# A limit on the bytes of transfers in flight, plain fp32 loads of the first inputs, and mixer weights cast straight into tiles

## The chip, the cores and the metric

The program runs on all 8 cores of one Trainium2 chip. Each core works on its own 2 of the 16 sequences and reads its own copy of the weights; nothing passes between cores. A time is the device time of one execution in microseconds (us), taken at the slowest core. The number to forecast is the median of such times.

## The reference

The reference is a trunk of two layers on x of shape 16 x 2048 x 1024, in fp32. Each layer adds half of a SwiGLU block, a token mixer, and half of a second SwiGLU block:

```python
for l in range(DEPTH):                                   # DEPTH = 2
    x = x + 0.5 * swiglu(rms_norm(x, ffn1_norm[l]), ffn1_w1[l], ffn1_w3[l], ffn1_w2[l])
    x = x + token_mixing(rms_norm(x, mix_norm[l]), w_in[l], ..., group_norm[l], w_out[l])
    x = x + 0.5 * swiglu(rms_norm(x, ffn2_norm[l]), ffn2_w1[l], ffn2_w3[l], ffn2_w2[l])
# swiglu(h, w1, w3, w2) = (silu(h @ w1) * (h @ w3)) @ w2, inner width 2816
```

`token_mixing` projects with `w_in`, splits the columns into four groups of heads (native sparse attention with a compressed, a selected and a windowed branch; a gated short convolution; sliding-window attention with sinks; a multi-scale pooling), normalises each group and projects with `w_out`.

## The kernel before

**Work and its units.** Activations lie with features on partitions and tokens on the free axis. A feed-forward (FFN) unit is one SwiGLU block on 1024 tokens of one sequence; there are 16 units, listed in `FL` (four of the first block of layer 0, then for each sequence two of its second block and two of the next layer's first, and so on). A mixer chunk is the token mixer on 512 tokens; there are 16, listed in `ML`. A unit's products are done in blocks of 512 columns with a scheme of seven products for each 2x2 block product (`PROD`, `prod`, L703): 11 "pairs" (columns of w1 and w3) and, per group of the inner width, four blocks of w2 (`dcq`). The sums of weight blocks that the scheme needs are formed on VectorE (DVE) by `wsum` (L659), those of activations by `tops` (L695).

**Weights.** They come as fp32 in DRAM (`w13r`, `w2r`, `winr`, `cw1r`, `wtokr`, `woutr`). An FFN tile of 128 x 2048 is cast to fp16 at first use by a DMA of GpSimd's queue (`prep`, L635), one sum is put in, and it is stored to a DRAM scratch (`s13`, `s2`) by SyncE's queue (L644); later units load it from there (`wload`, L670). The mixer's weights of a layer are cast from DRAM to a DRAM scratch (`hin`, `hcw`, `htok`, `hout`) by 32 DMAs on GpSimd's queue in `mix_scratch`, 6 of them spread over FFN unit 1 and the others over unit 2 of layer 0; what is not yet issued when the layer's first chunk begins is issued there in one go (`SCR.pop` in `mstream`). Every chunk then loads its tiles from that scratch (`proj` L860, `compress` L893, `chunk` L994, L995 and L1133).

**Inputs.** `norm` loads eight tiles of 128 x 512 tokens through GpSimd's queue, which casts them to fp16 (L605), squares them on ScalarE (L608), sums them by matmuls with ones (L610), and scales the tiles in place on DVE (L617). The first block of layer 0 reads `xT`; the result accumulates in `yT`, to which `ycopy` (L1358) copies `xT` by 32 DMAs from DRAM to DRAM on SyncE's queue.

**What sets the order.** The code first writes down all operations in program order, the FFN stream and the mixer stream interleaved by the table `MIX` (pairs of FFN units done and chunks done) and the work totals `tot`. `Graph.schedule` then runs a list scheduler over them with estimated durations: each engine takes the ready operation with the smallest key, within a look-ahead (`ahead`, `ahead_dma`, or an operation's own `look`) and within pools of tile slots. Operations that read PSUM get a smaller key by `bonus` or `bonusx`. DMAs are modelled as one pipe of `bw` bytes per us with a latency `hlat` (SyncE) or `slat` (GpSimd). The resulting order is fixed in the program; at run time only semaphores hold it back, and each queue issues strictly in its order. The pools matter below: 130 tiles "1" (128 x 520 fp16), 20 tiles "2" (128 x 1024 fp16 or 128 x 512 fp32), 7 tiles "4" (128 x 2048 fp16, a weight tile each).

## Time and profile before

| | |
|---|---|
| median of three runs, us | 4719.72 (lowest 4717.16) |
| profiled execution | 4709.09 us; its slowest core (core 3) spans 4708.1 us |
| other cores | 4670.8 to 4697.4 us |
| TensorE (PE) busy, core 3 | 4552.1 us, 97% of the span |
| DVE, ScalarE (ACT), GpSimd (POOL) busy | 3098.3, 3088.8, 897.1 us |
| HBM read and written | 630.62 and 256.43 MB |

How to read it: the profiled execution is 10.6 us, or 0.2%, faster than the median shown, so a saving read from it is taken off the median as it stands. PE's idle time in the profile is what a change of order can win or lose; the granted clock tells where PE ran below full speed.

### The profile page before, as it was taken

Reading aid. Unit: us, or ns where it says so; the run is one execution under the profiler, and the core shown is the slowest. Engines: PE = TensorE matmul, PEld = TensorE weight load, DVE = VectorE, ACT = ScalarE, POOL = GpSimd, SP = SyncE. Lnnn points to the kernel's source line nnn. Section 1 sums busy time; section 2 is a strip of 40 time slices with the busy share of each in tenths; the row PEclk is TensorE's granted clock in tenths of the full one; section 3 lists DMA queues with packets and bytes.
Section 4 is the critical chain, followed back from the end, with each engine's and each line's share of the span. In section 5 each row is a group of like instructions: output and inputs, shape, how many; then the busy total and the mean of one; then the engine's idle time right before and its main releaser. Section 6 shows DMA issues by size and latency. Waiting matters only on the chain.

```text
span 4708.1 us, 86069 instructions; the slowest of 8 cores (4670.8 to 4708.1 us)
## 1 busy us (share of the span) xinstructions
PE 4552.1 (97%) x25524; PEld 2109.0 (45%) x25524; DVE 3098.3 (66%) x7506; ACT 3088.8 (66%) x5770; POOL 897.1 (19%) x1328
## 2 busy tenths in 40 slices
PE   6999799999999999999999999999999999999989
PEld 2444344444444444444444444444444444444434
DVE  4747377657667667676667666766667776766553
ACT  3434277678686686786957586858685867767342
POOL 2021212021213112222112111121212221111101
PEclk8899899999999999999999999999999999999999
DMA  9898965766899649997567665674659996655634
GB/s 164 168 181 198 155 167 116 174 131 132 170 213 184 160 104 205 187 209 155 145 142 174 118 155 112 146 166 79 166 124 187 182 192 144 156 111 123 136 81 94
DMA packets 357974, 718.87 MB, mean 153 GB/s; under 512 B 37744, under 2 KB 149232, under 8 KB 356464
## 3 DMA queue, kind: packets, MB, share of 16 engines
q0 software_dynamic: 173392, 297.07, 44.0%
q1 hardware_dynamic: 184128, 416.29, 27.5%
q8 instruction: 219, 3.59, 0.3%
q14 instruction: 235, 1.93, 0.1%
HBM read 630.62 MB, written 256.43 MB: 188 GB/s over the span
## 4 chain that ended last, share of the span: by engine, by line
PE 87%; DMA 4%; DVE 3%; issue 2%; ACT 2%; another core or an unknown queue 1%; POOL 0%; SPq 0%; DVEq 0%; ACTq 0%; POOLq 0%
PE ps L703 62%; PE ps L864 8%; PE ps L1137 5%; PE ps L1152 4%; PE ps L1165 2%; DMA M<-s 2%; PE ps L610 1%; PE ps L1001 1%; DMA M<-w13r 1%; PE ps L1246 1%; PE ps L928 1%; DMA M<-yT 1%; DMA M<-w2r 0%; PE ps L968 0%
## 5 line engine op out<-in xcount | busy, mean ns | idle before, releaser
L703 PE MATMUL ps<-M 128*128 128x512 f16 x14784 | 3457.7, 383 | 84.0 <-DVE M L750 19.8
L703 PEld LDWEIGHTS ps<-M 128*128 128x128 f16 x14784 | 1414.4, 98 | 1782.9 <-issue 296.5
L659 DVE TENSOR_TENSOR M<-M 128x512 f16<-128x512 f16 (+1 forms) x1780 | 689.2, 411 | 181.7 <-DMA M<-s 83.4
L750 DVE TENSOR_TENSOR M<-M,ps 128x512 f16<-128x512 f32 x704 | 481.9, 685 | 458.8 <-PE ps L703 322.2
L802 POOL DMA_DIRECT2D yT<-M x464 | 400.7, 874 | 1685.3 <-ACT M L790 751.9
L754 ACT COPY M<-ps 128x512 f32<-128x512 f32 x704 | 411.2, 585 | 265.6 <-PE ps L703 259.9
L1155 ACT ACTIVATE M<-ps 128x512 bf16<-128x512 f32 x824 | 456.3, 604 | 38.6 <-PE ps L1152 34.6
L864 PE MATMUL ps<-M 128*128 128x512 f16 x1920 | 445.6, 379 | 0.4 <-DVE MS L1173 0.4
L710 ACT COPY ps<-ps 128x512 f32<-128x512 f32 x468 | 273.0, 583 | 249.5 <-PE ps L703 197.4
L695 DVE TENSOR_TENSOR M<-M 128x512 f16<-128x512 f16 x960 | 386.4, 421 | 35.3 <-DVE M L695 1.0
L742 DVE TENSOR_TENSOR M<-M,ps 128x512 f16<-128x512 f16 x352 | 240.8, 684 | 206.6 <-PE ps L703 203.0
L796 DVE SCALAR_TENSOR_TENSOR M<-ps,M 128x512 f32<-128x512 f32 x232 | 159.7, 689 | 232.6 <-PE ps L703 196.0
L864 PEld LDWEIGHTS ps<-M 128*128 128x128 f16 x1920 | 185.7, 98 | 217.4 <-issue 2.6
L617 DVE SCALAR_TENSOR_TENSOR M<-M,GN 128x512 f16<-128x512 f16 x384 | 263.8, 744 | 28.4 <-ACT M L624 27.8
L790 ACT ACTIVATE M<-ps 128x512 f32<-128x512 f32 x232 | 138.7, 599 | 217.8 <-PE ps L703 205.5
L1152 PE MATMUL ps<-M 96*128 96x512 f16 x824 | 273.6, 380 | 2.3 <-DVE M L1185 2.2
L738 ACT ACTIVATE M<-M 128x512 f16<-128x512 f16 x352 | 219.0, 631 | 82.4 <-DVE M L750 81.6
L734 ACT ACTIVATE M<-ps 128x512 f16<-128x512 f32 x352 | 209.5, 596 | 77.9 <-PE ps L703 74.6
L605 POOL DMA_DIRECT2D M<-yT x320 | 188.3, 667 | 343.5 <-PE ps L703 112.6
L608 ACT ACTIVATE M<-M 128x512 bf16<-128x512 f16 x384 | 228.6, 630 | 25.2 <-DMA M<-xT 11.7
L1165 PEld LDWEIGHTS ps<-M 128*128 128x128 bf16 x3296 | 176.4, 97 | 144.5 <-issue 28.3
L1137 PE MATMUL ps<-M 128*128 128x512 f16 x1024 | 235.7, 382 | 1.9 <-DVE M L1353 1.8
(152 smaller groups left out, 3983.7 us busy)
## 6 DMA issues: line engine op xcount, KB each, us to landing
M<-s SPq DMA_DIRECT2D x360, 512.0 KB, 4.9
yT<-M POOLq DMA_DIRECT2D x592, 256.0 KB, 7.8
s<-M SPq DMA_DIRECT2D x120, 512.0 KB, 8.0
M<-hin SPq DMA_DIRECT2D x240, 256.0 KB, 6.7
M<-w13r POOLq DMA_DIRECT2D x88, 512.0 KB, 13.0
M<-yT POOLq DMA_DIRECT2D x320, 128.0 KB, 7.5
M<-hout SPq DMA_DIRECT2D x128, 256.0 KB, 6.6
M<-w2r POOLq DMA_DIRECT2D x40, 512.0 KB, 9.9
```

What stands on the lines that cost most here:

```text
L659: op("dve", lambda e, o_=o_, a_=a_, b_=b_, al=al: e.tensor_tensor(out=wap(W, o_, w), in0=wap(W, a_, w), in1=wap(W, b_, w), op=al), reads=[ ...
L695: op("dve", lambda e, o_=o_, x_=x_, y_=y_: e.tensor_tensor(out=p1(o_)[:, 0:512], in0=p1(x_)[:, 0:512], in1=p1(y_)[:, 0:512], op=ALU.subtract),
L703: r = e.matmul(ps(bk)[:], lhsT=wap(w, pos, 128, j * 128), rhs=p1(B[n, k0 + j])[:, 0:512], start=start and j == 0, stop=stop and j == nk - ...
L710: op("act", lambda e: e.copy(out=ps(dst)[:], in_=ps(src)[:]), reads=[src], writes=[dst], dur=0.57)
L750: op("dve", lambda e: e.tensor_tensor(out=p1(dst)[:, 0:512], in0=p2f(t), in1=ps(bk)[:], op=ALU.add), reads=[t, bk], writes=[dst], dur=t_dv ...
L754: op("act", lambda e: e.copy(out=p2f(t), in_=ps(bk)[:]), reads=[bk], writes=[t], dur=0.6)
L802: op("pool", lambda e: e.dma_start(out=yT[s, :, dc, t0:t0 + 512], in_=p2f(o), accum_op=ALU.add), reads=[o], writes=[kY[s][dc][2 * u + hf]] ...
L864: r = e.matmul(ps(bk)[:], lhsT=p2(t)[:, kc * 128:(kc + 1) * 128], rhs=p1(xn[kc])[:, 0:512], start=kc == 0, stop=kc == 7, skip_group_check= ...
L1137: r = e.matmul(ps(bk)[:], lhsT=p2(wo)[:, kc * 128:(kc + 1) * 128], rhs=yap(kc), start=n == 0, stop=n == 7, skip_group_check=True)
L1152: op("pe", lambda e: e.matmul(ps(sbk)[:], lhsT=kap(), rhs=p4(Q)[0:kk, b * 512:(b + 1) * 512], start=True, stop=True, skip_group_check=True ...
L1155: op("act", lambda e: e.activation(out=p1b(et)[:, 0:512], in_=ps(sbk)[:], func=AF.Exp, scale=0.125), reads=[sbk], writes=[et], dur=0.65, t ...
L1165: r = e.matmul(ps(pb)[:, h * 65:(h + 1) * 65], lhsT=p1b(et)[:, h * 128:(h + 1) * 128], rhs=p1(V)[:, (kt % 4) * 130 + vi * 65:(kt % 4) * 13 ...
```

## The change

Five things change, and with them the order of the whole program.

1. The scheduler keeps a log of DMA bytes in the order of issue. A DMA is issued only when the bytes issued after some earlier DMA, its own included, would otherwise reach `win` = 5 MB: it then waits for that earlier DMA to land, in the model and by a semaphore on the chip. Bytes are those of the `dma` argument, which is the fp32 size for a cast.
2. For the units 0 to 2 (`XWIDE`: sequence 0, and the first 1024 tokens of sequence 1) `norm` loads `xT` as fp32 into tiles "2" by SyncE's queue, without a cast; squares and scaling read the fp32 tile and the scaled result goes to the fp16 tile. The loads of `norm` get a look-ahead of 400.
3. `mix_scratch` is gone. `mload` casts a mixer tile from the fp32 weights into the tile that the first chunk uses (GpSimd's queue) and stores it from there to the scratch (SyncE's queue); later chunks load it as before. `chunk` does the same with `wtokr`.
4. The scheduler's numbers: `ahead` 600 to 400, `hlat` 3 to 4, `slat` 6 to 4.5, `bonusx` 0 to 100, and shorter durations and larger byte counts for some DMAs.
5. The interleaving: the last point of `MIX` by which the mixer is done moves from 14.6 to 14.4 FFN units of 16, and the totals from 200 and 73 to 203 and 75.5.

```diff
-        self.ahead = 600
+        self.ahead = 400
-        self.hlat = 3.0
-        self.slat = 6.0
+        self.hlat = 4.0
+        self.slat = 4.5
+        self.win = 5000000.0
-        self.bonusx = 0
+        self.bonusx = 100
...
+                if c.dma:
+                    while dptr < len(dlog) and dcum + c.dma - dlog[dptr][0] >= self.win:
+                        dptr += 1
+                    q = dlog[dptr - 1][1] if dptr else None
+                    if q is not None and q.end > tnow + 1e-9:
+                        heapq.heappush(pe_, (q.end, c.i, c))
+                        continue
+                    throt[c.i] = q
...
+            if o.dma:
+                if throt.get(o.i) is not None:
+                    ex.add(throt[o.i])
+                dcum += o.dma
+                dlog.append((dcum, o))
...
-MIX, PREP, MS1 = ((2.0, 0.0), (5.0, 4.4), (14.6, 16.0)), (0, 1), 6
+LOOKX, XWIDE, XDMA = 400, (1, 2), 450e3
+MIX, PREP = ((2.0, 0.0), (5.0, 4.4), (14.4, 16.0)), (0, 1)
...
+            wide = src is xT and (s, c) < XWIDE
+            xf = [tile("2") for _ in range(8)] if wide else dst
+            xa = (lambda t: p2f(t)) if wide else (lambda t: p1(t)[:, 0:512])
             for kc in range(8):
-                op("pool", lambda e, kc=kc: e.dma_start(out=p1(dst[kc])[:, 0:512], in_=src[s, :, kc, c * 512:(c + 1) * 512]),
-                   reads=[kY[s][kc][c]], writes=[dst[kc]], dur=0.8, dma=262144)
+                op("sp" if wide else "pool", lambda e, kc=kc: e.dma_start(out=xa(xf[kc]), in_=src[s, :, kc, c * 512:(c + 1) * 512]),
+                   reads=[kY[s][kc][c]], writes=[xf[kc]], dur=0.45 if wide else 0.6, dma=262144 if wide else XDMA, look=LOOKX)
...
-        def mix_scratch(l):
...
+        def mload(l, kind, k, ap, wr, part=None):
+            src, dst, key = dict(hin=(winr, hin, kHIN), hout=(woutr, hout, kHOUT), hcw=(cw1r, hcw, kHCW))[kind]
+            nb = 128 * src.shape[-1] * 2
+            if (l, kind, k) in minscr:
+                op("sp", lambda e: e.dma_start(out=ap(), in_=dst[l, k]), reads=[key[l][k]], writes=[wr], dur=0.45, dma=nb, look=LOOKM)
+            else:
+                minscr.add((l, kind, k))
+                op("pool", lambda e: e.dma_start(out=ap(), in_=src[l, k]), writes=[wr], dur=0.6, dma=2 * nb, look=LOOKM)
+                op("sp", lambda e: e.dma_start(out=dst[l, k], in_=ap()), reads=[wr], writes=[key[l][k]], dur=0.45, dma=nb)
...
-                        spread(ms[:MS1], [1])
-                        spread(ms[MS1:], [2])
...
-                for f in SCR.pop(l, ()):
-                    f()
...
-        tot = [200.0 * max(1, len(FL)), 73.0 * max(1, len(ML))]
+        tot = [203.0 * max(1, len(FL)), 75.5 * max(1, len(ML))]
```

In the listings of the order below, lines of the changed kernel carry its own numbers: L627 is `norm`'s load (L605 before), L639 its scaling (L617), L657 and L659 the casts of FFN weights (L635, L637), L666 their stores (L644), L681 `wsum` (L659), L717 `tops` (L695), L725 `prod` (L703), L764 and L772 the readers of its PSUM banks (L742, L750), L824 the accumulation into `yT` (L802), L876 and L1022 the mixer casts, L1167 the projection with `w_out` (L1137), L1366 and L1378 the last steps of the pooling and of the group norm (L1336, L1348), L632 the sum of squares (L610).

**The program's start.** DVE's first instructions before, in which L659 are sums of weight tiles (four per tile) and L617 the scaling of the input tiles:

```order
L573 MEMSET EPSB 128x1
L576 MEMSET ONES 128x128
L659 TENSOR_TENSOR M<-M 128x512 x2
L617 SCALAR_TENSOR_TENSOR M<-M,GN 128x512 x8
L659 TENSOR_TENSOR M<-M 128x512 x2
L617 SCALAR_TENSOR_TENSOR M<-M,GN 128x512 x6
L742 TENSOR_TENSOR M<-M,ps 128x512
L617 SCALAR_TENSOR_TENSOR M<-M,GN 128x512 x2
L695 TENSOR_TENSOR M<-M 128x512 x16
L659 TENSOR_TENSOR M<-M 128x512 x5
```

DVE's first instructions now:

```order
L592 MEMSET EPSB 128x1
L595 MEMSET ONES 128x128
L681 TENSOR_TENSOR M<-M 128x512 x20
L639 SCALAR_TENSOR_TENSOR M<-M,GN 128x512 x8
L681 TENSOR_TENSOR M<-M 128x512 x8
L764 TENSOR_TENSOR M<-M,ps 128x512
L639 SCALAR_TENSOR_TENSOR M<-M,GN 128x512 x8
L717 TENSOR_TENSOR M<-M 128x512 x16
L772 TENSOR_TENSOR M<-M,ps 128x512 x3
```

The sums of five weight tiles stand ahead of the first eight scalings, and those of two more ahead of the second eight; before, it was half a tile and half a tile more.

SyncE's queue at the start before:

```order
L574 DMA GN<-fnorm 128x48
L1358 DMA yT<-xT 128x1024 x3
L644 DMA s<-M 128x2048
L1358 DMA yT<-xT 128x1024 x5
L644 DMA s<-M 128x2048 x19
L1358 DMA yT<-xT 128x1024 x2
L644 DMA s<-M 128x2048 x2
```

SyncE's queue now:

```order
L593 DMA GN<-fnorm 128x48
L627 DMA M<-xT 128x512 x9
L666 DMA s<-M 128x2048
L627 DMA M<-xT 128x512 x7
L666 DMA s<-M 128x2048
L1388 DMA yT<-xT 128x1024
L666 DMA s<-M 128x2048 x3
L1388 DMA yT<-xT 128x1024 x3
L666 DMA s<-M 128x2048
```

The sixteen input loads stand at the head of this queue, two stores among them, and the copies of `xT` to `yT` follow behind; GpSimd's queue now begins with 22 casts of weight tiles in a row.

**The start of the mixer.** GpSimd's queue where the first chunk of layer 0 begins, before (`hcw`, `htok`, `hin` and `hout` are the DRAM scratch, L802 the accumulation of FFN outputs):

```order
L851 DMA hcw<-cw1r 16x4096 x2
L802 DMA yT<-M 128x512
L851 DMA hcw<-cw1r 16x4096 x2
L852 DMA htok<-wtokr 32x8576
L848 DMA hin<-winr 16x8192 x3
L802 DMA yT<-M 128x512
L848 DMA hin<-winr 16x8192
L802 DMA yT<-M 128x512
L848 DMA hin<-winr 16x8192 x4
L802 DMA yT<-M 128x512
L848 DMA hin<-winr 16x8192 x6
L854 DMA hout<-woutr 16x8192 x8
```

The same place now:

```order
L876 DMA M<-cw1r 128x512 x5
L824 DMA yT<-M 128x512 x3
L659 DMA M<-w2r 128x4x384
L824 DMA yT<-M 128x512 x3
L876 DMA M<-winr 128x1024
L876 DMA M<-cw1r 128x512 x2
L824 DMA yT<-M 128x512
L876 DMA M<-cw1r 128x512
L1011 MEMSET M 128x8
L1022 DMA M<-wtokr 128x268
L1011 MEMSET M 128x8
L1048 MEMSET M 32x512
```

The 27 casts of the first listing, close behind each other, are replaced by those of the compression weights, of a projection tile and of the token projection; most projection tiles come later, and the eight of `w_out` come last.

**The end of the last mixer chunk.** PE's last instructions before:

```order
L864 MATMUL ps<-M 128x512 x16
L703 MATMUL ps<-M 128x512 x7
L864 MATMUL ps<-M 128x512 x16
L1348 MATMUL ps<-M,ONES 128x512 x2
L610 MATMUL ps<-M,ONES 128x512 x8
L1336 MATMUL ps<-M,PRB 128x512 x2
L1348 MATMUL ps<-M,ONES 128x512 x2
L703 MATMUL ps<-M 128x512 x8
L1137 MATMUL ps<-M 128x512 x64
L703 MATMUL ps<-M 128x512 x12
L610 MATMUL ps<-M,ONES 128x512 x8
L703 MATMUL ps<-M 128x512 x904
```

PE's last instructions now:

```order
L1167 MATMUL ps<-M 128x512 x16
L725 MATMUL ps<-M 128x512 x52
L1167 MATMUL ps<-M 128x512 x8
L725 MATMUL ps<-M 128x512 x4
L1167 MATMUL ps<-M 128x512 x8
L725 MATMUL ps<-M 128x512 x496
L632 MATMUL ps<-M,ONES 128x512
L725 MATMUL ps<-M 128x512 x4
L632 MATMUL ps<-M,ONES 128x512 x5
L725 MATMUL ps<-M 128x512 x4
L632 MATMUL ps<-M,ONES 128x512 x10
L725 MATMUL ps<-M 128x512 x1120
```

Products of an FFN unit (L725) now stand between the pieces of the projection with `w_out`, and 496 of them between it and the sums of squares of the last unit's inputs (L632). Before, 20 products stood between the chunk's last pooling step and the last sums, and then the unit's 904.

## Rows read from the trace of the kernel before

**Rows 1.** The page's head and its first section: busy us, share, instructions.

```profile
span 4708.1 us, 86069 instructions; the slowest of 8 cores (4670.8 to 4708.1 us)
...
PE 4552.1 (97%) x25524; PEld 2109.0 (45%) x25524; DVE 3098.3 (66%) x7506; ACT 3088.8 (66%) x5770; POOL 897.1 (19%) x1328
```

**Rows 2.** Second section, busy share of the DMA engines in 40 slices of 117.7 us.

```profile
DMA  9898965766899649997567665674659996655634
```

**Rows 3.** Core 3 by stretch: length, busy us (instructions), granted clock, DMA share, GB/s.

```profile
0.00:73.00 73.00, 32.11 (x88) 9.22 (x88) 27.03 (x62) 22.99 (x36) 13.59 (x29) 0.83 0.96 168
73.00:300.00 227.00, 226.78 (x914) 96.15 (x915) 131.45 (x293) 88.00 (x149) 42.25 (x67) 0.86 0.87 164
300.00:480.00 180.00, 171.81 (x778) 75.95 (x777) 119.23 (x266) 80.76 (x141) 28.89 (x50) 0.98 0.88 200
480.00:590.00 110.00, 81.05 (x460) 36.59 (x459) 39.13 (x79) 31.97 (x57) 21.93 (x38) 0.85 0.99 155
590.00:960.00 370.00, 353.94 (x2066) 165.53 (x2065) 258.39 (x663) 252.88 (x507) 63.18 (x91) 0.98 0.66 150
960.00:4430.00 3470.00, 3441.44 (x20129) 1617.86 (x20128) 2380.07 (x5847) 2512.27 (x4716) 697.30 (x1015) 1.00 0.72 154
4430.00:4515.00 85.00, 58.55 (x234) 23.65 (x233) 42.96 (x84) 31.05 (x47) 16.28 (x22) 0.82 0.50 90
4515.00:4708.00 193.00, 186.42 (x863) 84.01 (x861) 100.01 (x216) 68.90 (x119) 13.67 (x16) 1.00 0.37 91
```

**Rows 4.** The same view of core 0, two stretches.

```profile
73.00:300.00 227.00, 215.21 (x966) 94.89 (x969) 139.63 (x315) 94.45 (x160) 42.79 (x68) 0.96 0.96 183
...
480.00:590.00 110.00, 75.95 (x440) 35.48 (x440) 37.99 (x80) 34.85 (x72) 17.53 (x32) 0.83 0.93 164
```

**Rows 5.** Timeline of the start, core 3: start, length, instruction, idle time before, releaser.

```profile
34.73 4.06 DVE L617 SCALAR_TENSOR_TENSOR M<-M,GN 128x512 f16<-128x512 f16 x6 [7.33 <-ACT M L624]
...
49.00 12.30 PE L703 MATMUL ps<-M 128*128 128x512 f16 x48 [2.48 <-DVE M L695]
...
57.24 2.44 DVE L659 TENSOR_TENSOR M<-M 128x512 f16<-128x512 f16 x7 [1.25 <-DMA M<-w13r]
...
71.71 0.76 DVE L659 TENSOR_TENSOR M<-M 128x512 f16<-128x512 f16 x2 [6.26 <-DMA M<-w13r]
...
73.22 2.29 PE L703 MATMUL ps<-M 128*128 128x512 f16 x5 [11.91 <-DVE M L750]
```

**Rows 6.** DMA queues, 0 to 300 us: packets, MB, share of 16 engines.

```profile
q0 software_dynamic: 14055, 26.71, 63.5%
q1 hardware_dynamic: 6512, 22.49, 25.7%
```

**Rows 7.** DMA queues and issues, 480 to 600 us: packets, MB, share; KB each, landing.

```profile
q0 software_dynamic: 2614, 9.67, 67.1%
...
hin<-winr POOLq DMA_DIRECT2D x14, 256.0 KB, 35.7
...
hout<-woutr POOLq DMA_DIRECT2D x8, 256.0 KB, 59.8
...
htok<-wtokr POOLq DMA_DIRECT2D x1, 536.0 KB, 17.9
```

**Rows 8.** Timeline of PE, 480 to 640 us.

```profile
546.06 8.29 PE L703 MATMUL ps<-M 128*128 128x512 f16 x28 [5.68 <-DMA M<-s]
565.71 9.68 PE L703 MATMUL ps<-M 128*128 128x512 f16 x32 [11.36 <-DVE M L742]
585.68 1.69 PE L901 MATMUL ps<-PRB,M 64*128 64x1 f16 x61 [10.29 <-DMA M<-htok]
```

**Rows 9.** Timeline of PE, 4340 us to the end.

```profile
4454.76 0.38 PE L1336 MATMUL ps<-M,PRB 128*128 128x512 f16 x1 [2.25 <-DVE M L1333]
...
4481.64 2.79 PE L703 MATMUL ps<-M 128*128 128x512 f16 x8 [2.61 <-ACT ps L710]
...
4503.56 8.44 PE L703 MATMUL ps<-M 128*128 128x512 f16 x32 [12.66 <-DVE M L695]
```

More of the change, by code:

```diff
@@ L522, in build_program @@
         kPRB = [fix("PRB")] * L
-        kHTOK = [fix("H") for _ in range(L)]
+        kHTOK = [[fix("H"), fix("H")] for _ in range(L)]
         kHIN = [[fix("H") for _ in range(15)] for _ in range(L)]
@@ L843, in build_program @@
         MX = {}
-        def mix_scratch(l):
-            r = []
-            for k in range(15):
-                r.append(lambda k=k: op("pool", lambda e: e.dma_start(out=hin[l, k], in_=winr[l, k]), writes=[kHIN[l][k]], dur=0.8, dma=600e3, look=LOOKC))
-                if k == 0:
-                    for m in range(8):
-                        r.append(lambda k=m: op("pool", lambda e: e.dma_start(out=hcw[l, k], in_=cw1r[l, k]), writes=[kHCW[l][k]], dur=0.8, dma=300e3, look=LOOKC))
-                    r.append(lambda: op("pool", lambda e: e.dma_start(out=htok[l], in_=wtokr[l]), writes=[kHTOK[l]], dur=0.8, dma=1200e3, look=LOOKC))
-            for k in range(8):
-                r.append(lambda k=k: op("pool", lambda e: e.dma_start(out=hout[l, k], in_=woutr[l, k]), writes=[kHOUT[l][k]], dur=0.8, dma=600e3, look=LOOKC))
-            return r
+        minscr = set()
+        def mload(l, kind, k, ap, wr, part=None):
[7 more added lines that the diff above has]
+                op("sp", lambda e: e.dma_start(out=dst[l, k], in_=ap()), reads=[wr], writes=[key[l][k]], dur=0.45, dma=nb)
         def proj(l, name, xn, bk):
             t = tile("2")
-            k = WIN_T.index(name)
-            op("sp", lambda e: e.dma_start(out=p2(t), in_=hin[l, k]), reads=[kHIN[l][k]], writes=[t], dur=0.45, dma=262144, look=LOOKM)
+            mload(l, "hin", WIN_T.index(name), lambda: p2(t), t)
             def f(e):
@@ L993, in chunk @@
             wt, wt2 = tile("4"), tile("1")
[L994 to L995 removed]
+            for t, c0, c1, q in ((wt, 0, 1876, p4), (wt2, 1876, 2144, p1)):
+                n = c1 - c0
+                if (l, "htok", c0) in minscr:
+                    op("sp", lambda e, t=t, c0=c0, c1=c1, q=q: e.dma_start(out=q(t)[:, 0:c1 - c0], in_=htok[l][:, c0:c1]), reads=[kHTOK[l][c0 > 0]], writes=[t],
+                       dur=0.45, dma=256 * n, look=LOOKM)
+                else:
+                    minscr.add((l, "htok", c0))
+                    op("pool", lambda e, t=t, c0=c0, c1=c1, q=q: e.dma_start(out=q(t)[:, 0:c1 - c0], in_=wtokr[l][:, c0:c1]), writes=[t],
+                       dur=0.6, dma=512 * n, look=LOOKM)
+                    op("sp", lambda e, t=t, c0=c0, c1=c1, q=q: e.dma_start(out=htok[l][:, c0:c1], in_=q(t)[:, 0:c1 - c0]), reads=[t], writes=[kHTOK[l][c0 > 0]],
+                       dur=0.45, dma=256 * n)
             for b in range(4):
@@ L1132, in chunk @@
                 wo = tile("2")
-                op("sp", lambda e, dc=dc, wo=wo: e.dma_start(out=p2(wo), in_=hout[l, dc]), reads=[kHOUT[l][dc]], writes=[wo], dur=0.45, dma=262144, look=LOOKM)
+                mload(l, "hout", dc, lambda wo=wo: p2(wo), wo)
                 def f(e, wo=wo, bk=bk):
@@ L1398, in build_program @@
         BG = {}
-        SCR = {}
-        def once(fs):
-            ran = set()
-            def one(k):
-                if k not in ran:
-                    ran.add(k)
-                    fs[k]()
-            return [lambda k=k: one(k) for k in range(len(fs))]
         def spread(fs, idx):
@@ L1428, in build_program @@
                 p = pos[l, 1]
-                if do_mixer:
-                    ms = once(mix_scratch(l))
-                    SCR[l] = ms
-                    if l == l0:
-                        spread([lambda x=x: one_prep(l0, 0, *x) for x in tiles_of() if x[0] == "2"], [1])
-                        spread(ms[:MS1], [1])
-                        spread(ms[MS1:], [2])
-                    else:
-                        spread(ms, list(range(pos[l, 0], pos[l, 0] + 2)))
+                if l == l0 and nseq > 1:
+                    spread([lambda x=x: one_prep(l0, 0, *x) for x in tiles_of() if x[0] == "2"], [1])
                 if l == l0:
```

21 lines of the change are left out of this document (10 added, 11 removed).

## The prediction

> **What bounds the kernel now.** The page's first section comes first: TensorE (PE) is busy 4552.1 of 4708.1 us [rows 1]. No other engine is near it, so what a new order can save is PE's idle time, 156 us, and time lost at a lower granted clock. The table by stretches shows where they lie [rows 3]. In the 3470 us from 960 to 4430 PE idles 28.6 us, at clock 1.00: 0.8%, nothing to win. The loss sits at four places: the first 73 us (40.9 idle), 300 to 480 us (8.2), 480 to 590 us (29.0, at clock 0.85) and 4430 to 4515 us (26.5, at 0.82); 590 to 960 us adds 16.1. In the first three the DMA engines are 0.88 to 0.99 busy; in the last only 0.50. So the beginning is ruled by transfers and the end by a chain of dependent steps.
>
> The timelines of these places say what was late. At the start PE ran 48 products from 49.00 us and then stood 11.91 us until 73.22, since DVE waited for cast weight tiles (57.24, another wait between, 71.71) [rows 5]. Near 550 us it stood three times, 5.68, 11.36 and 10.29 us: twice for FFN weights that come back from the scratch, once for the mixer's [rows 8]. The DMA view of that stretch shows what they queued behind: 14 casts to `hin`, 8 to `hout` and one to `htok` [rows 7]. At the end three of the waits are 2.25, 2.61 and 12.66 us, behind vector steps [rows 9]: the last chunk ends with nothing beside it, and the last FFN unit cannot begin before its inputs are summed and scaled.
>
> **The start.** Prices first. From 0 to 300 us the queue of casts took 63.5% of 16 engines for 26.71 MB, which is 300 x 0.635 = 190.5 us, or 140 KB per us; the plain queue 77 us for 22.49 MB, 292 KB per us [rows 6]. (Bytes are those written.) A weight tile of 0.524 MB costs 3.74 us of all engines. The sixteen input loads of a unit cost 2.10 / 0.140 = 15.0 us as casts and, twice the bytes, 4.19 / 0.292 = 14.4 us as plain loads. The move to SyncE's queue therefore saves half a microsecond of DMA time; what it changes is the order of landing. In the new order DVE forms the sums of five weight tiles before the first scaling and of seven before the second eight. It must wait for 7 x 3.74 + 14.4 = 40.6 us of transfers, some 43 us with first issue and landing. Then come eight scalings at 0.68 us each (six took 4.06 [rows 5]) and the first sums of inputs: PE runs without a break from about 51 us, and 16 products stand ahead of that, 3.5 us at the 216 ns of full clock (186.42 us for 863 instructions in the last stretch [rows 3]). Its run thus starts as if at 47.5 us. Before, 68 products stood ahead of 73.22, 4 each on five occasions and the 48, 14.7 us: as if at 58.5. That is 11 us better. Against it: the seven tile slots are then full and the DRAM copies of `xT`, which ran before PE's run, come into it, so some of the 11 is lost again. Bounds: 0, if the DMA bytes of unit 0 alone set its end (they are the same to half a microsecond), and 23, if PE could run from 35. I take 6, nearer to the lower end, as the stretch from 73 to 300 us is already at DMA share 0.87 on this core and 0.96 on core 0 [rows 3, 4].
>
> These cores differ there: core 3 was granted 0.86, core 0 0.96, yet core 0 gained only 52 instructions, 11 us, since it waited where core 3 was slow [rows 3, 4]. A core at the lower clock keeps that loss in the new order, so I count nothing for it.
>
> A rule of the Trainium skill speaks against a gain here: *DMA: Bandwidth & Descriptors*, section "Issuing engines are not separate DMA queues", says that DMAs of all issuing engines end on the same 16 engines and interleave. The two prices above agree with it; by the rule alone this term would be 0 and the forecast 4664.
>
> **From 300 to 480 us.** The inputs of units 1 and 2 leave the queue of casts and are issued earlier, with a look-ahead of 400. PE idles 8.2 us here [rows 3]; I take 5 off, bounds 0 and 8.
>
> **The mixer's start.** The casts to `hin`, `hout` and `htok` of the window are 22 x 0.262 + 0.549 = 6.3 MB. The cast queue moved 9.67 MB in 0.671 x 120 = 80.5 us there, 120 KB per us [rows 7]: 53 us of all engines. By 590 us the new order needs only the compression weights (8 tiles of 0.131), the first projection tile and the token projection, 1.86 MB or 15 us, and it stores them once, 6 us at the plain price. Some 30 us of transfers move out of this stretch to 600 to 960 us, where the share is 0.66 [rows 3]: 370 x 0.34 = 126 us of engine time are free there and hide them. The three waits sum to 27.3 us [rows 8]. Where PE came out of them it ran slowly: 28 products in 8.29 and 32 in 9.68 us, 5.0 more than at 216 ns. So 27.3 + 5.0 = 32.3 us are at stake, out of 29.0 idle and the clock. New here: each first use waits for a cast with nothing loaded ahead of it. An issue of the old casts needed 17.9 us to land for the smallest group, 35.7 and 59.8 for the others, in the crowd [rows 7]. I charge 4, for the first use or two. Gain 28, bounds 12 (one wait of 11.36 and the clock's share remain, and one cast is late) and 32. In layer 1 the same move finds PE without idle time and is worth nothing either way.
>
> **The end.** The rest of the last chunk now lies among products of an FFN unit, and 196 products of unit 14 (1120 less a unit's 924) follow the sums of squares, 42 us, which cover the scaling and input sums that PE stood 12.66 us for. All 26.5 us of idle time between 4430 and 4515 can go [rows 3], and the slow clock after them: 32 products in 8.44 us [rows 9] are 1.5 over, and I put the stretch at 4, an estimate from this row. I take 28 of 30.5; bounds 20 and 30.5. DVE and ACT are at 0.66 [rows 1], so the chunk's steps fit beside a unit.
>
> **What is added.** The limit of 5 MB: with FP32 sizes a weight tile counts 1.05 MB, so it is five tiles, 5 x 3.74 = 19 us of transfers at the price above. A queue that always has 19 us of work lets the engines idle only if landing takes as long. But SyncE and GpSimd issue in order: where one waits for a landing, FFN weight loads stand behind it on SyncE's queue, and accumulations into `yT` on GpSimd's, which free the tiles that ACT and DVE write. The mixer also has to fit in 9.4 units from the fifth to 14.4 instead of 9.6, 2% denser, with 28.6 us of idle time there to begin with. The trace of before has no such wait; the nearest price is a wait of PE for a late weight tile, 11.36 us [rows 8]. Bounds: a gain of 5 (urgent loads no longer queue behind others) and a loss of 3 such waits, 34. I take a loss of 5, nearer to nothing, because most slices past 960 us show the DMA engines at 4 to 7 tenths [rows 2], so the limit seldom holds. The new priority of PSUM readers (`bonusx`) and the shorter look-ahead I cost at nothing: PE is 99% busy where they act.
>
> **Sum.** 6 + 5 + 28 + 28 - 5 = 62 us off the profiled 4709.1 gives 4647; off the median, 10.6 higher, 4719.7 - 62 = 4658. Forecast: 4658 us, 1.3% faster.
>
> **Rivals.**
> *Bytes decide.* The start, and units 1 and 2, are held by DMA time that the change leaves as it is, and the mixer's weights come late instead of others. For it: shares of 0.88 to 0.99 to 590 us [rows 3]; against it: 30 us of transfers do leave the stretch. Then the end alone gains, with its 28, and a third of the mixer's start, 9: 4683.
> *Everything closes.* The start gains its full 23, the mixer's start and the end their bounds, 32 and 30, and half of the 44.7 us of idle time between 590 and 4430 goes, as loads are no longer crowded: 23 + 8 + 32 + 30 + 22 = 115, 4605. For it: the limit is what keeps urgent loads from queueing; against it: from 960 to 4430 PE has no more than 28.6 us to give, and no price above shows DMA time saved at the start.
> *The limit stalls the queues.* In bursts, where the DMA engines are full (11 of 40 slices show a 9, eight of them past 960 us [rows 2]), SyncE stands for a landing of GpSimd's, and an FFN weight tile behind it comes late by a wait like 11.36 us [rows 8]. It decides from six of them, 68 us, where the gain is used up; with one in each of the 12 units after the first four it is 136 us against 67 gained (62 without the 5 charged), 4789, 1.5% slower than before; over 2%, 4814, takes fifteen.
>
> **How the numbers follow.** Forecast 0.55, bytes decide 0.2, everything closes 0.17, the limit stalls 0.08. The range reaches from 4600 (just beyond everything closing) to 4710 (bytes decide, with two late tiles more); beyond it lie perhaps 0.06 below and 0.1 above. A run of this kernel tells 2%, 94 us, from no change: faster than 4625 is everything closing and the upper part of the forecast, 0.2; over 4814 only the worst of the last rival, 0.02; the rest, 0.78, lies within.
>
> **What would show it.** Start: the second eight scalings on DVE at 43 to 48 us and unbroken products from near 51. Mixer: 480 to 590 us of idle under 8 us, no three waits, and casts spread to 800 us. End: no wait over 2 us after the projection with `w_out`, clock 1.00 up to the last product. Limit: no wait of PE for an FFN weight tile from 960 us on over 5 us. I am wrong if the DMA share stays near 1 past 600 us with PE waiting, or if PE's idle time from 960 to 4430 grows beyond 45 us.

## The result and the profile after

The time fell by 1.1%: the ratio to the kernel before is 0.9891, 95% interval [0.9862, 0.9921], which on the 4720 us of before is 4669 us (4655 to 4682), against a forecast of 4658. The two times behind it are 4662.98 and 4673.88 us. By the measure of 2% that is no change. Executions in which the cores of a die were granted a lower clock are left out here; on the two chips of the last eight experiments every execution was of that kind, the kernel before's included, so their times carry no verdict, and their idle times are set beside those of the same chip.

Below is the page of the kernel after (its head and the DMA slices), to be read beside [rows 1, 2].

```profile
span 4661.9 us, 86720 instructions; the slowest of 8 cores (4636.2 to 4661.9 us)
...
PE 4518.3 (97%) x25524; PEld 2101.8 (45%) x25524; DVE 3088.4 (66%) x7506; ACT 3050.7 (65%) x5742; POOL 874.4 (19%) x1282
...
DMA  9998796767998759886588666664776898646554
```

PE idles 143.6 us (4661.9 less 4518.3). The table by stretches of its slowest core has the same columns as [rows 3, 4]: length, busy time of PE, PE's weight loads, DVE, ACT and POOL, granted clock, DMA share, GB/s.

```profile
0.00:73.00 73.00, 21.71 (x51) 6.29 (x52) 27.85 (x63) 18.66 (x28) 4.62 (x12) 0.89 0.98 203
73.00:300.00 227.00, 212.42 (x965) 94.12 (x964) 134.24 (x293) 93.52 (x161) 33.50 (x51) 0.98 0.92 174
300.00:480.00 180.00, 178.64 (x828) 80.54 (x827) 122.46 (x270) 84.34 (x147) 26.73 (x43) 1.00 0.90 213
480.00:590.00 110.00, 96.25 (x568) 44.84 (x567) 58.24 (x153) 62.98 (x110) 16.74 (x27) 0.92 0.71 153
590.00:960.00 370.00, 361.66 (x2109) 170.39 (x2108) 254.39 (x625) 249.70 (x503) 79.95 (x114) 0.99 0.83 169
960.00:4385.00 3425.00, 3377.71 (x19766) 1584.09 (x19764) 2336.41 (x5769) 2439.03 (x4621) 685.57 (x1004) 1.00 0.73 153
4385.00:4470.00 85.00, 84.92 (x394) 38.13 (x393) 55.99 (x124) 34.88 (x58) 13.62 (x16) 1.00 0.63 132
4470.00:4662.00 192.00, 184.99 (x857) 83.42 (x855) 98.88 (x214) 67.57 (x117) 13.66 (x16) 1.00 0.38 91
```

The same table for all cores, cut at 4370 and 4560 instead, gives these medians of PE's idle time over the eight cores, in us. They are the currency of all that follows; the experiments' (e1 to e4, described below) come from the same view of each.

| stretch, us | before | after | e1 | e2 | e3 | e4 |
|---|---|---|---|---|---|---|
| 0 to 73 | 40.8 | 50.5 | 38.5 | 48.8 | 49.3 | 36.8 |
| 73 to 300 | 8.2 | 12.0 | 42.7 | 12.3 | 9.9 | 6.5 |
| 300 to 480 | 2.4 | 2.8 | 1.8 | 2.5 | 4.0 | 9.8 |
| 480 to 590 | 34.5 | 13.1 | 11.8 | 13.7 | 5.6 | 1.8 |
| 590 to 960 | 9.2 | 7.8 | 8.9 | 8.6 | 1.0 | 6.8 |
| 960 to 4370 | 32.1 | 46.1 | 43.8 | 52.1 | 45.7 | 41.2 |
| 4370 to 4560 | 26.2 | 0.1 | 0.1 | 0.5 | 28.8 | 0.1 |
| 4560 to the end | 6.7 | 6.7 | 6.5 | 6.6 | 6.3 | 6.8 |
| median span of a core | 4692.8 | 4650.1 | 4680.6 | 4662.0 | 4671.3 | 4624.9 |

The median core is 42.7 us shorter. Idle time gives 21 of it: 21 at the mixer's start and 26 at the end, less 10 at the start, 4 to 300 us and 14 in the middle. The other 22 us are PE's busy time, for the same number of products. The granted clock fits this: it went from 0.80-0.85 to 0.92 or more between 480 and 590 us, from 0.90-0.92 to 1.00 between 4370 and 4560, and over the whole span from 0.987 to 0.992 (middle of the eight cores).

**The start became worse.** The timeline of the first 90 us of the core above answers to [rows 5]: start, length, instruction, and in brackets the idle time before it and what ended it.

```profile
1.53 10.61 SPq L627 DMA_DIRECT2D M<-xT  x9
...
11.13 1.82 DVE L681 TENSOR_TENSOR M<-M 128x512 f16<-128x512 f16 x4 [9.77 <-DMA M<-w13r]
11.27 0.63 ACT L630 ACTIVATE M<-M 128x512 bf16<-128x512 f32 x1 [3.96 <-DMA M<-xT]
...
15.85 1.82 DVE L681 TENSOR_TENSOR M<-M 128x512 f16<-128x512 f16 x4 [2.90 <-DMA M<-w13r]
16.03 0.63 ACT L630 ACTIVATE M<-M 128x512 bf16<-128x512 f32 x1 [4.13 <-DMA M<-xT]
...
20.39 1.82 DVE L681 TENSOR_TENSOR M<-M 128x512 f16<-128x512 f16 x4 [2.71 <-DMA M<-w13r]
20.84 0.63 ACT L630 ACTIVATE M<-M 128x512 bf16<-128x512 f32 x1 [4.18 <-DMA M<-xT]
...
39.06 1.28 ACT L630 ACTIVATE M<-M 128x512 bf16<-128x512 f32 x2 [3.22 <-DMA M<-xT]
...
42.04 5.39 DVE L639 SCALAR_TENSOR_TENSOR M<-M,GN 128x512 f16<-128x512 f32 x8 [10.78 <-ACT M L646]
...
44.93 5.11 PE L725 MATMUL ps<-M 128*128 128x512 f16 x12 [3.86 <-DVE M L639]
...
59.19 5.39 DVE L639 SCALAR_TENSOR_TENSOR M<-M,GN 128x512 f16<-128x512 f32 x8 [3.37 <-ACT M L646]
...
68.75 9.46 PE L725 MATMUL ps<-M 128*128 128x512 f16 x32 [11.39 <-DVE M L717]
```

Read DVE and ACT in pairs: at 11.13 and 11.27, 15.85 and 16.03, 20.39 and 20.84 (and twice more, to 29.9) DVE gets a weight tile and ACT an input tile within 0.6 us of each other. Nine input loads had been issued by 12.14 us, and yet they land one for each weight tile, 4.6 us apart. The DMA view of the first 22 us (queue: packets, MB written, share) shows the same in packets. Of the plain queue's 859, 144 belong to the table of norm gains (the whole of this queue in the same view of e4), so it moved 715 packets of inputs beside 597 of casts:

```profile
q0 software_dynamic: 597, 2.22, 65.9%
q1 hardware_dynamic: 859, 1.34, 25.0%
```

The eighth input is squared at 39.06, the first eight are scaled from 42.04 and the second eight from 59.19. PE's unbroken run begins at 68.75 with 20 products ahead of it, 4.3 us at 216 ns: as if at 64.4, where before it was 58.5.

**The mixer's start.** The timeline of PE there answers to [rows 8], and the DMA view of 480 to 600 us (queue: packets, MB, share) to [rows 7].

```profile
491.52 1.69 PE L922 MATMUL ps<-PRB,M 64*128 64x1 f16 x61 [2.19 <-DMA M<-cw1r]
...
498.99 1.04 PE L949 MATMUL ps<-M 64*128 64x31 f16 x29 [4.68 <-issue]
...
500.57 1.44 PE L725 MATMUL ps<-M 128*128 128x512 f16 x3 [0.54 <-DMA M<-s]
```

```profile
q0 software_dynamic: 4270, 6.30, 41.0%
q1 hardware_dynamic: 4941, 11.68, 30.5%
```

The three long waits are gone; the first compression weight, cast with nothing loaded ahead, costs 2.19. The queue of casts moved 6.30 MB where it moved 9.67. The last cast of a mixer weight of this layer (`w_out`) is issued at 653.5 us.

**The end.** The timeline of PE from 4300 us answers to [rows 9]: 1109 products without a break of 2 us, and one wait of 0.94.

```profile
4410.45 2.32 PE L632 MATMUL ps<-M,ONES 128*128 128x512 bf16 x10
4412.61 239.85 PE L725 MATMUL ps<-M 128*128 128x512 f16 x1109
4653.40 2.54 PE L725 MATMUL ps<-M 128*128 128x512 f16 x11 [0.94 <-DVE M L818]
```

**The middle.** PE's waits from 960 to 4385 us (us in total, times, longest) have no load of an FFN weight tile among them, on any core. One tile of the mixer came late, and the rest are many waits of 1 to 3 us.

```profile
PE ps L885 <- DMA M<-hin: 5.7, 1, 5.7
PE ps L725 <- DVE M L818: 3.2, 4, 1.5
PE ps L725 <- DVE M L772: 3.1, 5, 1.9
```

### The profile page after: what moved, and what is told of

Its sections match the earlier page's. It is cut to its first block, busy times and chain, and to the rows that moved or that the text cites. A ratio compares the mean times of both kernels' runs of the same rounds, so it can differ in the third digit from the quotient of the medians.

```text
span 4661.9 us, 86720 instructions; the slowest of 8 cores (4636.2 to 4661.9 us)
## 1 busy us (share of the span) xinstructions
PE 4518.3 (97%) x25524; PEld 2101.8 (45%) x25524; DVE 3088.4 (66%) x7506; ACT 3050.7 (65%) x5742; POOL 874.4 (19%) x1282
## 4 chain that ended last, share of the span: by engine, by line
PE 85%; DMA 6%; DVE 4%; issue 3%; ACT 2%; POOL 0%; SPq 0%; DVEq 0%; ACTq 0%; POOLq 0%
PE ps L725 61%; PE ps L885 8%; PE ps L1167 4%; PE ps L1182 4%; PE ps L1195 2%; DMA yT<-M 2%; PE ps L632 1%; DMA M<-xT 1%; PE ps L1031 1%; DVE M L639 1%; DMA M<-s 1%; DMA M<-w2r 1%; DVE M L717 1%; PE ps L949 1%; PE ps L1276 1%
## 5 line engine op out<-in xcount | busy, mean ns | idle before, releaser
L725 PE MATMUL ps<-M 128*128 128x512 f16 x14784 | 3422.9, 380 | 54.5 <-DVE M L772 13.2
L725 PEld LDWEIGHTS ps<-M 128*128 128x128 f16 x14784 | 1409.0, 98 | 1730.8 <-issue 170.0
L681 DVE TENSOR_TENSOR M<-M 128x512 f16<-128x512 f16 (+1 forms) x1780 | 691.8, 412 | 130.7 <-DMA M<-s 53.8
L772 DVE TENSOR_TENSOR M<-M,ps 128x512 f16<-128x512 f32 x704 | 481.5, 685 | 435.6 <-PE ps L725 320.8
L824 POOL DMA_DIRECT2D yT<-M x464 | 400.3, 884 | 1697.2 <-ACT M L812 826.8
L717 DVE TENSOR_TENSOR M<-M 128x512 f16<-128x512 f16 x960 | 388.3, 424 | 34.3 <-DVE M L717 1.1
L764 DVE TENSOR_TENSOR M<-M,ps 128x512 f16<-128x512 f16 x352 | 240.9, 684 | 208.6 <-PE ps L725 206.5
L639 DVE SCALAR_TENSOR_TENSOR M<-M,GN 128x512 f16<-128x512 f16 (+1 forms) x384 | 265.2, 745 | 21.4 <-ACT M L646 21.2
L627 POOL DMA_DIRECT2D M<-yT x320 | 181.6, 608 | 458.5 <-PE ps L725 60.1
L630 ACT ACTIVATE M<-M 128x512 bf16<-128x512 f16 (+1 forms) x384 | 228.1, 627 | 39.1 <-DMA M<-xT 34.8
L1167 PE MATMUL ps<-M 128*128 128x512 f16 x1024 | 233.7, 379 | 0.4 <-DVE M L1383 0.4
```

The source lines that it names most:

```text
L639: op("dve", lambda e, d=dst[kc], gi=gi, x=xf[kc]: e.scalar_tensor_tensor(out=p1(d)[:, 0:512], in0=xa(x), scalar=GN[:, gi:gi + 1], in1=p2f( ...
L681: op("dve", lambda e, o_=o_, a_=a_, b_=b_, al=al: e.tensor_tensor(out=wap(W, o_, w), in0=wap(W, a_, w), in1=wap(W, b_, w), op=al), reads=[ ...
L717: op("dve", lambda e, o_=o_, x_=x_, y_=y_: e.tensor_tensor(out=p1(o_)[:, 0:512], in0=p1(x_)[:, 0:512], in1=p1(y_)[:, 0:512], op=ALU.subtract),
L725: r = e.matmul(ps(bk)[:], lhsT=wap(w, pos, 128, j * 128), rhs=p1(B[n, k0 + j])[:, 0:512], start=start and j == 0, stop=stop and j == nk - ...
L772: op("dve", lambda e: e.tensor_tensor(out=p1(dst)[:, 0:512], in0=p2f(t), in1=ps(bk)[:], op=ALU.add), reads=[t, bk], writes=[dst], dur=t_dv ...
L824: op("pool", lambda e: e.dma_start(out=yT[s, :, dc, t0:t0 + 512], in_=p2f(o), accum_op=ALU.add), reads=[o], writes=[kY[s][dc][2 * u + hf]] ...
```

## The experiments

All diffs are against the changed kernel unless another is named. e1 to e4 ran on one chip, e5 to e8 on a second, e9 to e12 on a third.

**e1: units 1 and 2 and unit 0 loaded as casts again.**

```diff
-LOOKX, XWIDE, XDMA = 400, (1, 2), 450e3
+LOOKX, XWIDE, XDMA = 400, (0, 0), 450e3
```

> The changed kernel with all input loads back on GpSimd's queue as casts. Theory (the plain loads of the start land in lockstep with the weight casts, one input tile per weight tile every 4.6 us, and that costs the start 6 to 9 us): the eighth input tile is squared by 20 us instead of 39, PE's idle time in the first 73 us falls from 50 to 41, some 4 us come back in units 1 and 2, the time is 3 to 8 us below the changed kernel. Rival (the byte limit holds the loads back, whatever their queue): the eighth input tile stays past 30 us and the time is the same within 3 us.

The ratio to the kernel before on that chip is 0.9964 [0.9934, 0.9994]. That is slower than the changed kernel (0.9891), not the 3 to 8 us faster that was expected. In one queue, the eighth input was squared at 17.18 us and the first 73 us idled 38.5, as expected. But from 73 to 300 us the idle time rose to 42.7. The windows of its slowest core (columns as above) and its waits from 73 to 300 us show with what:

```profile
0.00:73.00 73.00, 31.47 (x96) 10.12 (x97) 29.68 (x67) 25.27 (x38) 14.16 (x30) 0.79 0.90 141
73.00:300.00 227.00, 182.99 (x797) 77.90 (x796) 126.66 (x279) 76.23 (x133) 34.35 (x55) 0.91 0.83 159
```

```profile
PE ps L725 <- DMA M<-w2r: 29.0, 4, 8.8
```

GpSimd's queue shows how (first line from the changed kernel, the others from e1):

```profile
220.41 0.53 POOL L657 DMA_DIRECT2D M<-w2r  x1 [6.05 <-PE ps L632]
223.06 0.90 POOL L824 DMA_DIRECT2D yT<-M  x1 [29.47 <-ACT M L812]
231.37 0.56 POOL L657 DMA_DIRECT2D M<-w2r  x1 [0.29 <-issue]
```

The inputs of unit 1 now lie among this queue's weight casts, the last two around the first cast of `w2r`. Only three casts of `w2r` come before the first accumulation into `yT`; in the changed kernel seven do, the last at 220.41. The fourth stands behind that accumulation, for whose data the queue waited 29.47 us, and is issued at 231.37. So plain loads cost the start 12 us and are worth some 30 us between 73 and 300 us, through the order of GpSimd's queue. I had expected only the first, and a gain of some 4 us in units 1 and 2.

**e2: no limit on bytes in flight.**

```diff
-        self.win = 5000000.0
+        self.win = 5e12
```

> The changed kernel with the limit of bytes in flight taken off (5 TB). Theory (the limit is worth little; the lockstep at the start comes from the two queues taking turns): SyncE issues the 16 input loads within 10 us, but they still land 4 to 5 us apart, the eighth past 35 us, and the whole time is within 10 us of the changed kernel. Rival (the limit paces the start, and it is what removed the waits at the mixer's start): the eighth input tile lands by 22 us, and PE idles 25 us or more between 480 and 590 us again, so the time rises by 10 to 25 us.

Its two times that count are 4667.38 and 4669.68 us, beside 4694.85 to 4730.05 for the kernel before on that chip. The timeline of its start (slowest core):

```profile
1.52 24.66 SPq L627 DMA_DIRECT2D M<-xT  x16
...
11.72 0.63 ACT L630 ACTIVATE M<-M 128x512 bf16<-128x512 f32 x1 [3.54 <-DMA M<-xT]
16.53 0.63 ACT L630 ACTIVATE M<-M 128x512 bf16<-128x512 f32 x1 [4.18 <-DMA M<-xT]
20.95 0.63 ACT L630 ACTIVATE M<-M 128x512 bf16<-128x512 f32 x1 [3.79 <-DMA M<-xT]
...
38.51 1.16 ACT L630 ACTIVATE M<-M 128x512 bf16<-128x512 f32 x2 [4.20 <-DMA M<-xT]
```

All sixteen loads are issued by 26.2 us (expected within 10) and still land 4 to 5 us apart: the limit does not pace them. The mixer's start is as closed without it (13.7). What it may be worth is the middle, 52.1 against 46.1, where PE without the limit waits once 11.2 us for sums of weight tiles, and at most the 12 us by which the median cores differ, though from separate measurements of the two kernels.

**e3: the interleaving as before.**

```diff
-MIX, PREP = ((2.0, 0.0), (5.0, 4.4), (14.4, 16.0)), (0, 1)
+MIX, PREP = ((2.0, 0.0), (5.0, 4.4), (14.6, 16.0)), (0, 1)
-        tot = [203.0 * max(1, len(FL)), 75.5 * max(1, len(ML))]
+        tot = [200.0 * max(1, len(FL)), 73.0 * max(1, len(ML))]
```

> The changed kernel with the old interleaving table (14.6) and work totals (200 and 73). Theory (the end was closed by the interleaving): PE stands 10 us or more for the last unit's inputs again, 24 to 30 us of idle time return in the last 300 us, the time rises by 20 to 30 us. Rival (the end was closed by the look-ahead and the new priorities): the end stays closed and the time is within 6 us of the changed kernel.

The ratio to before is 0.9967 [0.9936, 0.9998]. The median core is 21 us longer than the changed kernel's (20 to 30 were expected). The open end is back, 28.8 us of idle at a clock of 0.91, and PE waits 12.5 us once for sums of inputs, as in [rows 9] (slowest core):

```profile
4370.00:4560.00 190.00, 161.17 (x702) 69.61 (x703) 102.16 (x214) 74.21 (x122) 24.86 (x32) 0.91 0.46 99
```

So of the five changes it is the interleaving that closes the end. With the old one, 480 to 960 us idles 6.6 us, with the new one 20.9; but e4 below keeps the new one and idles only 8.6 there, so this is not the price of the interleaving by itself. The middle idles as much with either (45.7, 46.1), which speaks against the denser mixer as what it lost by.

**e4: the inputs of unit 0 as casts, those of units 1 and 2 plain.**

```diff
-            wide = src is xT and (s, c) < XWIDE
+            wide = src is xT and (0, 2) <= (s, c) < XWIDE
```

> The changed kernel with only unit 0's inputs as casts on GpSimd's queue; units 1 and 2 keep plain loads. Theory (lockstep at the start costs 6 to 9 us and the plain loads of units 1 and 2 cost nothing): idle time in the first 73 us falls to about 41, the time is 5 to 10 us below the changed kernel. Rival (unit 0 ends when its DMA bytes are through, whatever their order): the waits return between 73 and 300 us and the time is the same within 3 us.

Two times count, 4630.73 and 4661.4 us, ratio to before 0.9888 [0.9807, 0.9968]. The timeline of its start and the windows of its slowest core:

```profile
15.93 0.63 ACT L630 ACTIVATE M<-M 128x512 bf16<-128x512 f16 x1 [0.90 <-DMA M<-xT]
...
53.62 6.55 PE L725 MATMUL ps<-M 128*128 128x512 f16 x22 [9.86 <-DVE M L717]
```

```profile
0.00:73.00 73.00, 36.01 (x119) 12.32 (x120) 34.32 (x77) 27.54 (x43) 14.14 (x30) 0.81 0.95 164
73.00:300.00 227.00, 217.52 (x997) 97.11 (x996) 143.28 (x319) 96.26 (x166) 33.78 (x51) 0.99 1.00 201
...
480.00:590.00 110.00, 108.20 (x574) 50.08 (x572) 65.19 (x182) 80.52 (x142) 26.21 (x38) 0.98 0.71 143
```

The eighth input is squared at 15.93 us, inputs follow each other 1.5 us apart, and the last wait over 2 us ends at 53.62. The start idles 13.7 less than in the changed kernel, 73 to 300 us stays low, and 480 to 590 falls to 1.8 as well. The median core, 4624.9, is 37 us below e2's on the same chip and the lowest of all versions. But by the ratio to before (0.9888 beside 0.9891) it does not differ from the changed kernel, and the two were not timed on one chip, so the gain is not shown.

**e7: the first eight weight tiles cast by four DMAs of 512 columns each.**

```diff
-            if w == 512:
+            if w == 512 and which == "13" and (l, fi) == (0, 0) and q < 4:
+                for b in range(4):
+                    op("pool", lambda e, b=b: e.dma_start(out=p4(t)[:, b * 512:(b + 1) * 512], in_=src[:, b * 512:(b + 1) * 512]),
+                       writes=[(t, b)], dur=0.6, dma=262144)
+            elif w == 512:
```

> The changed kernel with the first eight weight tiles cast by four DMAs of 512 columns each in place of one of 2048, so that a packet of the cast carries a quarter of a weight tile's row. Theory (the two queues take turns packet by packet, and a packet of the cast was four times as large): four input tiles land per weight tile, the eighth is squared by 24 us in place of 39, unbroken products begin 8 us or more sooner, PE idles 40 to 44 us in the first 73, and the time is 5 to 12 us below the changed kernel. Rival (the engines share by time or bytes, or the limit paces the loads): the eighth input tile stays past 33 us and the time is within 3 us.

Every plain load of unit 0 is as in the changed kernel; the pieces of the casts beside them are smaller. The timeline of its start, and its queues in the first 22 us:

```profile
19.23 0.63 ACT L630 ACTIVATE M<-M 128x512 bf16<-128x512 f32 x1 [0.82 <-DMA M<-xT]
20.53 0.63 ACT L630 ACTIVATE M<-M 128x512 bf16<-128x512 f32 x1 [0.67 <-DMA M<-xT]
22.18 0.63 ACT L630 ACTIVATE M<-M 128x512 bf16<-128x512 f32 x1 [1.03 <-DMA M<-xT]
```

```profile
q1 hardware_dynamic: 1555, 2.61, 44.7%
q0 software_dynamic: 1233, 1.13, 43.7%
```

The eighth input is squared at 22.18, where e5 and e6 on the same chip have it at 36.54 and 37.21 and the changed kernel at 39.06. The first 73 us idle 42.7 (49.0 and 49.1 in e5 and e6). Both are within what was expected of queues that take turns. The packets agree: 1411 of inputs (1555 less 144) beside 1233 of casts, again nearly one for one, while the bytes of the casts are a quarter for each packet. The limit also let fewer casts go ahead, two tiles' worth by 6 us in place of four; that alone does not set the pace, since e2 has seven issued by then and the changed kernel four, at the same pace. Its times are 4894.13 to 4916.91 us and once 5098.46; that the whole run gains by it is not shown.

**e6 and e10: the scratch of the mixer's weights put back, on two chips.** The casts run from DRAM to DRAM again, six spread over unit 1 and the others over unit 2, and what is left is issued when the first chunk begins. The diff shows the calls; `mix_scratch` itself is put back too.

```diff
+                ms = once(mix_scratch(l))
+                SCR[l] = ms
+                if l == l0:
+                    spread(ms[:6], [1])
+                    spread(ms[6:], [2])
...
+                for f in SCR.pop(l, ()):
+                    f()
```

> The changed kernel with the mixer's weights cast from DRAM to the DRAM scratch again, ahead of the first chunk and in one go at its start, as before. Theory (the casts at first use closed the mixer's start): PE idles 28 us or more between 480 and 590 us again, 13 in the changed kernel, and the time rises by 15 to 22 us. Rival (the limit or the plain loads of units 1 and 2 closed it): idle time there stays under 18 us and the time is within 5 us.

> The kernel of e6_scratch once more, since its clock was low: the mixer's weights through the DRAM scratch in one go. Theory (casts at first use closed the mixer's start): PE idles 25 to 36 us between 480 and 590 us, 10 to 15 in the changed kernel, and the cores' spans are 12 to 22 us above the changed kernel's median of 4650. Rival (limit or plain loads closed it): under 18 us there, spans within 5 us.

PE's waits from 480 to 590 us in e6:

```profile
PE ps L725 <- DMA M<-s: 17.3, 1, 17.3
```

e10 has the same wait, 16.1 us. The stretch idles 25.2 us (13.5 in e5 beside it) and 18.4 (12.7 and 9.6 in e12 and e9 beside it). The same wait is 7.4 us in e5 and 7.3 in e12, without the scratch. The casts in one go thus lengthen a wait for an FFN weight behind them, one and not three, and add 6 to 12 us of idle time: 25 and 18 us in all, where e6 expected 28 or more and e10 25 or more, and the rival under 18. Neither the limit nor the plain loads are needed, as the rival had it: without the one the stretch idles 13.7 (e2), without the other 11.8 (e1).

**e8 and e11: the kernel before with the new totals alone**, 203 and 75.5.

```diff
-        tot = [200.0 * max(1, len(FL)), 73.0 * max(1, len(ML))]
+        tot = [203.0 * max(1, len(FL)), 75.5 * max(1, len(ML))]
```

> The kernel before with one line of the change: the work totals 203 and 75.5 in place of 200 and 73. Theory (the end was open because the mixer's total was too small, so that its last part was written down after nearly all of the FFN): idle time from 4370 us to the end falls from 33 to under 10 us, the start and the mixer's start stay as before, the time is 18 to 28 us below the kernel before. Rival (what is won at the end is lost in a denser middle): idle time between 960 and 4370 us grows by 15 us or more and the time is within 8 us of the kernel before.

> The kernel of e8_totals_only once more, since its clock was low: the kernel before with the new work totals alone. Theory (the totals close the end and cost nothing else): idle time from 4370 us to the end under 10 us, that from 960 to 4370 within 8 us of the 32 before, spans 18 to 28 us lower. Rival (what the end gains, a denser middle loses): 60 us or more idle between 960 and 4370, spans within 8 us of before.

The end closes on both chips: from 4370 us on PE idles 9.8 and 15.7 us, where the kernel before had 32.9 when its profile was taken. (The changed kernel has 6.8 there.) So the totals alone suffice. The times show no gain: the lowest are 4938.54 in e8 beside 4928.51 of before, and 5026.26 in e11 beside 4997.56. The middle idles 66.1 and 58.6, and on every core PE stands there once 11.7 to 12.1 us for sums of weight tiles, a wait that the profile of before lacks (0.6 in all). That leans to the rival, by which what the end gives is lost in the middle of that kernel. It stays open, as there is no profile of the kernel before on these chips.

**e5 and e12: the scheduler's numbers as before** (`ahead`, `hlat`, `slat`, `bonusx`).

```diff
-        self.ahead = 400
+        self.ahead = 600
-        self.hlat = 4.0
-        self.slat = 4.5
+        self.hlat = 3.0
+        self.slat = 6.0
-        self.bonusx = 100
+        self.bonusx = 0
```

> The changed kernel with the scheduler's old numbers (look-ahead 600, latencies 3 and 6, no priority for the second kind of PSUM readers). Theory (the numbers set the fine order between 960 us and the end of the mixer, where the changed kernel idles 46 us against 32 before): that idle time falls by 8 to 14 us, start and end stay as in the changed kernel, 10 us less in all. Rival (the denser mixer costs the 14 us, not the numbers): idle time there stays at 42 to 50 us and the time is within 4 us.

> The kernel of e5_old_numbers once more, since its clock was low: the changed kernel with the scheduler's old look-ahead, latencies and priorities. Theory (the denser mixer costs the middle, and the new numbers give part of it back): PE idles 56 to 70 us between 960 and 4370 us, 46 in the changed kernel, spans 8 to 20 us above its median of 4650. Rival (the numbers are what costs the middle): 30 to 38 us there, spans 8 to 14 us lower.

Inconclusive. The middle idles 63.0 and 56.8 us, above its neighbours on the same chips (38.2 in e7, 56.7 in e6; 32.3 in e9, 51.9 in e10), which speaks against the new numbers as the cause of its loss. The neighbours differ by up to 20 us among themselves, so no more can be read from it. The changed durations and byte counts of some DMAs were not put back in any run.

**e9: e4 once more.**

> The kernel of e4_u0_cast once more, for its time: unit 0's inputs as casts, the rest as in the changed kernel. Theory (lockstep at the start): PE idles 35 to 41 us in the first 73 and under 6 between 480 and 590; the time is 1.5 to 2.1% below the kernel before. Rival (the gain seen once was that chip's): the time is 0.9 to 1.3% below, as the changed kernel's was.

The start idles 37.7 us again, 11 less than with plain inputs on that chip (48.6 and 49.2). From 480 to 590 us PE idles 9.6, where under 6 was expected. Its lowest time, 4947.09, is under the lowest of before there, 4997.56, but its times reach 5441.34, too far apart for a verdict.

## Why the prediction was right, and where it was wrong

**Right in sum, and in two of three large terms.** The forecast took 62 us off; the ratio gives 51, the median core 43. Its likeliest case came: the mixer's start and the end gained, the middle stayed within the bounds. That the sum came so near is in part luck. By the table, the terms of the start, of 300 to 480 us and of the middle gave 28 us of loss (the 73 to 300 us counted with the start) where they promised 6 of gain. PE's busy time made up for part of it: it fell by 22 us, where the terms had priced 9 of slow clock (5.0 and 4).

**The end, 28 forecast.** 26.1 of idle went, and the clock rose to 1.00. Both signs came true: no wait over 0.94 us, and 1.00 up to the last product. e3 shows that the interleaving is the cause, e8 and e11 that the totals alone suffice.

**The mixer's start, 28 forecast.** 21.4 us of idle went, and the clock rose; 13.1 were left where I had named 8 as the sign. The three waits are gone, and the first uses wait 2.19 us at most for a cast. The sign of casts spread to 800 us did not come: the last is issued at 653.5, and the DMA share from 590 to 960 us rose from 0.66 to 0.83 without costing PE idle time. e6 and e10 show the direction: with the scratch a wait for a weight grows to 16 to 17 us. They bring back 6 to 12 of the 21 us, so the rest of the gain is not traced to one change. What was left idle, small waits of which the longest is 4.68 us, falls to 5.6 with the old interleaving (e3) and to 1.8 with unit 0's inputs as casts (e4); it hangs on the order of the whole program, which the forecast did not price.

**The start, 6 forecast: wrong in sign, and outside its bounds of 0 to 23.** PE's idle time in the first 73 us grew by 9.7 us, and the run began as if at 64.4 and not at 47.5. The step that failed is "It must wait for 7 x 3.74 + 14.4 = 40.6 us of transfers". It prices sixteen loads as bytes at the plain queue's rate. They ran beside the casts, and the two queues took turns: one input of 256 KB for one weight tile, every 4.6 us, so that by 40.3 us nine inputs had been squared and not sixteen. e2 rules out the limit as what paces them, e7 shows that the size of the cast beside them does (22.18 us for the eighth input, 36.54 and 37.21 beside it), and e4 gets 13.7 us back by putting them in the casts' own queue. The Trainium skill, *DMA: Bandwidth & Descriptors*, "Queues, rings and completion order", says that each engine serves the queues it has work for in turn, a packet of each at a time. The pairs at 11.13 and 11.27, 15.85 and 16.03 us and the 597 packets of casts beside 715 of inputs agree with it. The rule that the prediction cited, by which this term would be 0, is about bandwidth; the order in which things land is what cost here.

The late inputs then met a second delay: ACT's squares of the second eight stand behind copies that wait for PE, and two loads of ACT's function table, 1.28 us each, fall between 50 and 58 us. So the second scaling came at 59.19. How much of the 17 us between the scalings is this was only read from the timeline and not tested.

**From 300 to 480 us, 5 forecast.** Nothing was gained on the median core (2.4 to 2.8); the 8.2 of [rows 3] was that core's, the others idled 0 to 5.4. But the plain loads of units 1 and 2 do pay, earlier than the term says: without them 73 to 300 us idles 42.7 (e1). The kernel before did not show that: its queue had issued the inputs of unit 1 by 114 us, and the first cast of `w2r` only at 182.

**The middle, 5 of loss forecast, bounds -5 to 34.** 14 us of idle were lost: inside the bounds, but the 46.1 are over the 45 that the prediction gave as a sign of being wrong. It is not the limit (52.1 without it), and e3 speaks against the denser mixer (45.7 with the old one), though in the kernel before the new totals go with a middle of 58.6 and 66.1 (e8, e11). No load of an FFN weight comes late, so the limit does not stall SyncE's queue. What remains are the order that follows from everything else, and the numbers, of which e5 and e12 decide nothing. It is open.

**The rivals.** "Bytes decide" was nearer at the start (no gain, where 9.7 us were lost), for another reason, and had the mixer's start wrong. "Everything closes" failed at the start and in the middle. "The limit stalls the queues" did not happen.
